# First attention: two softmax maps combined by GpSimd in two operations, pipeline four blocks deep

## The reference, cut to what matters

```python
def block(b):
    qb = lax.dynamic_slice_in_dim(q, start, QBLK, axis=1)
    s = jnp.einsum("bqhcd,bkhcd->bhcqk", qb, k).astype(jnp.float32) * scale
    s = s - (slopes[:, None, None] * dist)[None, :, None]
    s = jnp.where(allowed, s, -jnp.inf)
    p = jax.nn.softmax(s, axis=-1)
    w = p[:, :, 0] - lam * p[:, :, 1]
    return jnp.einsum("bhqk,bkhe->bqhe", w.astype(v.dtype), v)
o = rms_norm(o, subln_g) * (1.0 - lam_init)
```

## Time and profile before

| what | value |
|---|---|
| median of 3 runs | 3153.79 us (3151.83 to 3155.02) |
| the profiled execution, its own time | 3162.36 us |
| its span | 3160.3 us |
| busy over the span: PE, DVE, ACT, POOL | 2893.4, 1606.5, 1296.9, 158.5 us |
| first scores of A on PE | 1868.02 us |
| last output of A through DVE and ACT | about 2007 us |

### The profile page before, as it was taken

One profiled execution on the slowest core, in us unless ns is written; L12 is line 12 of the kernel. 1 busy time (PEld: TensorE's weight loads), 2 busy tenths in 40 slices (PEclk: granted clock), 3 DMA queues, 4 the chain that ended last, 5 costly groups with the idle time before them and its releaser, 6 DMA issues.

```text
span 3160.3 us, 37729 instructions
## 1 busy us (share of the span) xinstructions
PE 2893.4 (92%) x13850; PEld 2053.0 (65%) x13858; DVE 1606.5 (51%) x3156; ACT 1296.9 (41%) x2426; POOL 158.5 (5%) x180
## 2 busy tenths in 40 slices
PE   7999999999996599999994988899999989989998
PEld 3454468588875466666663865576677775876677
DVE  1217546234356766666653548464642557536433
ACT  2201235233233445554534537543542547436421
POOL 0000000000000010000104100000000000000000
PEclk9999999999997799999997999999999999999999
DMA  9420000132335499999975200201012200100121
GB/s 356 154 80 0 27 27 1 54 107 84 142 117 213 165 345 366 368 363 365 361 256 145 80 15 13 54 28 41 15 54 107 93 14 20 62 17 18 54 80 54
DMA packets 176872, 388.56 MB, mean 123 GB/s; under 512 B 7236, under 2 KB 8292, under 8 KB 176464
## 3 DMA queue, kind: packets, MB, share of 16 engines
q1 hardware_dynamic: 158992, 322.98, 29.3%
q0 software_dynamic: 17584, 63.53, 6.1%
q10 hardware_dynamic: 144, 0.01, 0.0%
HBM read 354.98 MB, written 31.51 MB: 122 GB/s over the span
## 4 chain that ended last, share of the span: by engine, by line
PE 84%; DVE 5%; ACT 4%; DMA 3%; issue 2%; SPq 1%; POOLq 0%; POOL 0%; DVEq 0%; ACTq 0%
PE psum L294 20%; PE psum L709 7%; PE psum L711 7%; PE psum L710 7%; PE psum L1390 4%; PE psum L1272 4%; PE psum L1274 4%; PE psum L1273 4%; PE psum L1408 3%; PE psum L1218 3%; PE psum L1217 3%; PE psum L1216 3%; PE psum L1437 2%; PE psum L1485 2%; PE psum L1487 2%
## 5 line engine op out<-in xcount | busy, mean ns | idle before, releaser
L710 PE MATMUL psum<-ring_r,kctx_r 128*128 128x512 f32 (+1 forms) x544 | 213.8, 393 | 0.0
L710 PE MATMUL psum<-ring_r,cols_r 128*128 128x512 f32 (+1 forms) x544 | 211.4, 389 | 0.0
L1838 ACT ACTIVATE ring<-ring,att 128x256 f32<-128x256 f32 (+7 forms) x256 | 173.1, 677 | 66.1 <-DVE att L2423 66.1
L1390 PE MATMUL psum<-wide 64*128 64x512 f32 (+2 forms) x704 | 157.1, 530 | 21.9 <-DVE att L2423 19.0
L294 PE MATMUL psum<-hidden,ring 128*128 128x512 f32 x384 | 167.5, 597 | 6.0 <-DVE wide L2162 4.0
L2288 DVE TENSOR_TENSOR ring_r<-ring,pair_r 128x1024 fp32r<-128x1024 f32 x128 | 148.1, 1219 | 23.5 <-ACT pair_r L1733 23.5
L1273 PE MATMUL psum<-ring_r,wide_r 128*128 128x512 f32 x384 | 151.3, 394 | 0.0
L1408 PE MATMUL psum<-ident,ring 128*128 128x128 f32 x640 | 122.0, 298 | 26.8 <-ACT sel_wT L1850 16.1
L1408 PEld LDWEIGHTS psum<-ident,ring 128*128 128x128 f32 x640 | 69.6, 145 | 106.6 <-issue 70.9
L294 PEld LDWEIGHTS psum<-hidden,ring 128*128 128x128 f32 x384 | 73.4, 192 | 97.0 <-issue 94.7
L1216 PE MATMUL psum<-small_r,ring_r 128*128 128x512 f32 x320 | 125.8, 393 | 0.8 <-DVE pair L2178 0.8
(11 more groups left out here) (459 smaller groups left out, 6791.3 us busy)
## 6 DMA issues: line engine op xcount, KB each, us to landing
ring<-in_w_gate SPq DMA_DIRECT2D x64, 1024.0 KB, 9.1
ring<-in_w_up SPq DMA_DIRECT2D x32, 1024.0 KB, 9.8
hidden<-in_w_up SPq DMA_DIRECT2D x32, 1024.0 KB, 9.7
hidden<-in_w_down SPq DMA_DIRECT2D x32, 1024.0 KB, 7.3
pair<-in_w_down SPq DMA_DIRECT2D x32, 1024.0 KB, 7.4
ring<-in_w_ada SPq DMA_DIRECT2D x24, 1024.0 KB, 12.1
ring<-in_w_in SPq DMA_DIRECT2D x24, 1024.0 KB, 7.4
ring<-in_even_w_in SPq DMA_DIRECT2D x16, 1024.0 KB, 16.1
```

Source lines behind the costliest of these rows:

```text
L710: self.eng.matmul(outp, XHIGH[b][:, k, :], low[:, k, 0:wd], start=False, stop=False)
L1390: mm = pe.matmul(bank(2 * (q % 2) + h)[:, 0:n], qT2[row, c, span(b)], kT2[row, 0 if name == "C" else c, k:k + n], start=True, stop=not dia ...
L1838: act.activation(sv, sv, ACT.Exp, bias=nmx[:, q:q + 1], scale=-1.0, accum_out=esum[:, r:r + 1]).then_inc(S(name + "_e"), 1)
```

## The change

The line `LAG = 3` of the class goes; A has a lag of 4, the other attentions keep 3. `transposes`, both `empty`, and `outputs` of A therefore handle the block before the one they handled at the same step. Two buffers of 128x1024 in `ctx_hidden` are added, ten in all, and a block's maxima wait for the transposes of the block five before. In `weights`, DVE stops after the factor r1 (signal `A_r`). POOL waits for it, multiplies map 1 by r1 in place (`tensor_scalar`), waits for its own result (`A_scaled`), and adds the two maps (`tensor_tensor`), which signals `A_w`. POOL's DMAs for the strips of heads 2 and 3 stand between its blocks 7 and 8, and 15 and 16, instead of directly behind the first two. Two semaphores are shared with signals of an earlier stage. DVE also waits, from block 4 on, for its own output of the block four before (`A_o`), as the factor's column is used again.

```diff
-    LAG = 3
-
-        self.heads = 1 if p == "A" else 2
+        self.heads, self.LAG = (1, 4) if p == "A" else (2, 3)
...
+        share("ratio", [("nf_ms", {"": TT}), ("A_r", {"": ATT["A"].n})])
+        share("pooled", [("gained", {"": TT}), ("A_scaled", {"": ATT["A"].n})])
...
+        SBUFS["A"] += [ctx_hidden[:, i * D:(i + 1) * D] for i in range(2)]
...
-            return SBUFS[name][(2 * g + h) % 8]
+            return SBUFS[name][(2 * g + h) % len(SBUFS[name])]
...
+                    def combine(g):
+
+                        e0, e1 = (sbuf_of("A", g, h)[:, 0:at.pairs[g][3] * P] for h in range(2))
+                        r = 2 * (g % 4)
+                        pool.wait_ge(S("A_r"), before("A_r") + g + 1)
+                        pool.tensor_scalar(e1, e1, rinv[:, r + 1:r + 2], None, ALU.mult).then_inc(S("A_scaled"), 1)
+                        pool.wait_ge(S("A_scaled"), before("A_scaled") + g + 1)
+                        pool.tensor_tensor(e0, e0, e1, ALU.add).then_inc(S("A_w"), 1)
+
+                    if name == "A":
+                        for i in range(nb):
+                            pool.dma_start(BIAS["A"][i], a["strip_a"][i]).then_inc(S(f"A_bias{i}"), 16)
+                        for g in range(at.n):
+                            i = at.pairs[g][0] + 1
+                            if nb <= i < 4 and g == at.last[i - nb] + 1:
+                                pool.wait_ge(S("A_s"), before("A_s") + at.bias_uses(i - nb))
+                                pool.dma_start(BIAS["A"][i % nb], a["strip_a"][i]).then_inc(S(f"A_bias{i % nb}"), 16)
+                            combine(g)
+                        continue
...
-                        if g >= 4:
-                            i = at.turns[g - 4, min(h, at.heads - 1)]
+                        depth = len(SBUFS[name]) // 2
+                        if g >= depth:
+                            i = at.turns[g - depth, min(h, at.heads - 1)]
...
+                    if name == "A" and g >= 4:
+                        dve.wait_ge(S("A_o"), before("A_o") + g - 3)
...
-                    e0, e1 = (sbuf_of(name, g, h)[:, 0:nk * P] for h in range(2))
                     r1 = rinv[:, r + 1:r + 2]
-                    link(dve.tensor_scalar(r1, r1, nlam, esum[:, r:r + 1], ALU.mult, ALU.mult))
-                    dve.scalar_tensor_tensor(e0, e1, r1, e0, ALU.mult, ALU.add).then_inc(S("A_w"), 1)
+                    dve.tensor_scalar(r1, r1, nlam, esum[:, r:r + 1], ALU.mult, ALU.mult).then_inc(S("A_r"), 1)
```

More of the change, by code:

```diff
@@ L919, in _ @@
                 if t:
-                    pool.wait_ge(S("nf_ms"), t)
+                    pool.wait_ge(S("nf_ms"), before("nf_ms") + t)
                     pool.wait_ge(S("gained"), t)
@@ L948, in _ @@
                             pool.wait_ge(S(name + "_s"), before(name + "_s") + at.bias_uses((i - nb) // per))
-                        if name == "A":
-                            pool.dma_start(o, a["strip_a"][i]).then_inc(S(f"A_bias{i % nb}"), 16)
-                        elif name == "B":
+                        if name == "B":
                             pool.dma_start(o, scratch["ncum"][i].partition_broadcast(P)).then_inc(S(f"B_bias{i % nb}"), 16)
@@ L1940, in root @@
             def root(t):
-                act.wait_ge(S("nf_ms"), t + 1)
+                act.wait_ge(S("nf_ms"), before("nf_ms") + t + 1)
                 act.activation(stat[:, 24 + t:25 + t], stat[:, 48 + t:49 + t], ACT.Sqrt, bias=epsc[:, 0:1], scale=1.0 / D).then_inc(S("n3_rt"), 1)
```

## The result

The changed kernel takes 3174.18 us (median of 4 runs, 3166.94 to 3177.36) against 3154.22 of before: a ratio of 1.0058, 95% interval 1.0042 to 1.0075, so 13 to 24 us slower. A second measurement gave 1.0059 (1.0046 to 1.0071). The forecast was 3158, 4.3 us slower, with a range to 3169: right in sign, too small by a factor of more than four.

A forecast was written before the change was run, and what follows sets the result against it. PE was taken to set the pace before, POOL's serial combinations and pause after. First squares +5.2, +5.1 after head 1, +3.8 after head 2, last head +0.5: sum +4.3 us on 3153.8, said as 3158, range 3149 to 3169.

The forecast's parts named there:

- POOL's prices: For 128x1024, tensor_scalar 2.85 us and tensor_tensor 2.37; a combination over nk tiles 0.53 + 0.61 nk us, a head 26.1.
- POOL in series: In A, combinations run on one in-order POOL queue that PE's transposes wait for; sum +4.3 us, chance 0.76.
- The first squares: Head 0's first squares at 1913.6 instead of 1908.4, +5.2 us, with 3.1 us from the transposes to the squares.
- Head 1: Second head of A: a period of 31.4 us against 31.5 before.
- head 2: Third head of A: a period of 31.3 us, PE's own bound at the lower clock, against 32.6 before.
- last head: Last head of A, without a sixth block: 25.5 us to the squares against 25.0, +0.5.
- Then 6, 3, 5, 4 and 8 tiles, 18.4 us: After POOL's pause at a head's end, these five blocks run on to 27.7 us after the first square.
- The deeper pipeline: At a head's end the added lag gives POOL 7.7 us of work for a pause of over 12, nothing else.
- POOL keeps up: Rival: POOL's scaling is short here and PE sets the pace; near -4 us, 3150; chance 0.12.
- The pipeline gives the pause back: Rival: PE has a block more to work on while ACT squares; -7 us, 3146; chance 0.05.
- POOL holds DVE up: Rival: DVE's maxima are slowed beside POOL; up to +30 us, 3184 as an upper end; chance 0.07.
- the fixed share: Width-independent time of a POOL operation, taken as 0.18 us; with 0 the sum is +1.1, with 0.56 it is +11.

The follow-up runs named there:

- warm_after: The changed kernel with PE kept busy by matrix products of overwritten result while it waits at heads' starts and ends; 3164.1 us, 1.0033 to before.
- add_only: The changed kernel without POOL's multiplication by the factor, so the second map is added unscaled and the output differs; 3151.7 us, 0.9990 to before.
- spread_after: The changed kernel with ACT's squares computed one per step as outputs come, instead of all at the head's end; 3157.9 us, 1.0007 to before.
- pool_lag3: The changed kernel with a lag of 3 instead of 4 in A, all else kept; 3202.9 us, 1.0159 to before.
- dve_lag4: The changed kernel with the combination back on DVE as one operation, lag of 4 and ten buffers kept; 3158.7 us, 1.0027 to before.

## Why the prediction was wrong, point by point

**What bounds it, POOL's prices, POOL in series.** Right. Operations cost what was reckoned, POOL did not keep up, DVE was not held (0.69 us for 512 columns of the maxima beside POOL as without), and DVE's small new waits show in no row.

**The first squares, +5.2 us: measured +8.0** (from the first factor to head 0's root 43.0 us against 35.0). The step that failed is "from them to the squares ... I take 3.1". It was 4.8 (1909.28 to 1914.07), as PE came out of a wait of 2.9 us at the lower clock (0.66 over the stretch). Where the clock was 1.00, at the end of head 1 and in warm_after, the same way took 3.23 and 3.24 us. So what the term left out is the clock behind a wait that the change itself makes. The other part is a pause of 1.58 us at block 4 where I had POOL never pause.

**Head 1, -0.1: +2.6; head 2, -1.3: +0.9; last head, +0.5: +2.7.** POOL resumed 9.1 us after the first square; 9.3 was said. (It had paused 1.15 us before its block of 2 tiles already, whose factor I had called ready; that changed nothing, as ACT's return sets the next factor.) The step that failed is the next sentence, "Then 6, 3, 5, 4 and 8 tiles, 18.4 us", without a pause. The factor of the block of 3 tiles came 2.3 us too late. In front of it PE had, at half clock, seven transposes, the scores of one tile, one output and the eight transposes of the finished head (1.83 us), and only then the scores whose maxima DVE does before that factor. I had counted POOL and PE as two bounds and taken the larger; but while POOL is dry, PE's catching up is in series with it. With the pauses of 2.31 and 0.65 us these five blocks and the strip's issue took 21.7 us instead of 19.0. The last head has the same pause (2.63 us): the transposes of block 31 started 24.6 us after the first square of head 2 where I had 22.35, and from them to the squares it was 3.1 as said. That it is the length of POOL's work that makes heads 1 and 2 long is shown by add_only, where they are 2.5 and 2.4 us shorter (31.6 and 31.1). warm_after gives the clock's share (3 to 6 us in A), spread_after the whole pause's (12.5 us).

**The deeper pipeline, "all that it gives".** I let it give POOL work for the pause, which it did (pool_lag3: 32.8 us more without it), and priced its other effects at nothing. dve_lag4 shows 8.7 us, a term put at nothing without a reason. But it is no fixed price: add_only has the same lag, and its A is 2.2 us below before. In the changed kernel itself PE's wait for ACT stayed at 4.2 us, so that this sum is not simply part of the 14: DVE, freed of L2450, is no longer late with the last output by as much (2.56 us of ACT's wait in head 0, 1.46 later). Against the same lag with DVE, POOL costs 5.4 us in A (7.9 by the second profile), and 7.4 where the squares are spread. These 5.4 us lie in the first head (3.8) and the last (3.0); heads 1 and 2 are 0.6 and 0.9 us shorter with POOL than with DVE at this lag, so two different causes can make them as long.

**The rivals.** POOL keeps up: the add_only run shows what that would have been worth, 3151.7, near the 3150 said. The pipeline gives the pause back: no, PE's wait for ACT stayed at 4.2 us, and was 5.6 with the combination on DVE. POOL holds DVE up: no.

**The range.** It ended at 3169, 4 us above the upper end of the fixed share (+11, 3165). It had no room for an error of mechanism, and the one price that was uncertain, the fixed share, came out near where I had put it.

## What to carry to other kernels

When work moves to a slower engine in series with a pipeline, lay out the refill after each stall instruction by instruction, on one time axis for all queues: taking the larger of two engines' bounds misses that they wait for each other by turns. A deeper pipeline hides the latency of one step, but also moves every end-of-group action one step further from what it waits for; price both. Look for the stall first: here eight squares in a row on ACT cost more (5.3 us) than the change was worth even with POOL's work halved (2.2 us against before, the lag of 4 included).

## What the runs showed of the hardware that was not expected

GpSimd's multiplication by a column scalar is slower than its addition of two tensors at every width that A has: 2.84 against 2.34 us for 1024 columns, 0.60 against 0.46 for 128. A few products of no use (3.70 us of them in a wait of over 4) made the whole faster by 2 to 8 us in one kernel and, with three more in each head's other wait, by some 8 in the other, as PE came out of its wait at a granted clock of 1.00 instead of 0.5 to 0.7. And whether the clock falls around a short wait differs from one execution of a kernel to the next: with the same three waits of 1.3 to 1.6 us it was 1.00 behind them in one profile and 0.50 in the other, 2.4 us of the last head.
